# Seams of a two-layer transformer kernel cut by token tile, with the next stage's first two weight units multiplied in column halves

## What is computed

```python
for l in range(DEPTH):                       # DEPTH = 2
    # six modulation vectors per layer from silu(c) @ w_mod[l], for latents and for context
    h = rms_norm(x, g_pre_mix[l]) * (1 + sc1) + sh1
    y_lat, y_ctx = token_mixer(h, h_ctx, ...) # w_in, differential attention, gated linear attention, w_out
    x = x + gt1 * rms_norm(y_lat, g_post_mix[l])
    h = rms_norm(x, g_pre_ffn[l]) * (1 + sc2) + sh2
    f = swiglu(h, ffn_w1, ffn_w3, ffn_w2) if l == 0 else moe_ffn(h, router, moe_w1, moe_w3, moe_w2)
    x = x + gt2 * rms_norm(f, g_post_ffn[l])  # the context goes the same way in layer 0
```

## Time and profile before

| | |
|---|---|
| median of 3 runs | 2034.84 us (2032.96 to 2035.08) |
| the profiled execution | 2033.05 us |
| its span, first to last instruction | 2030.9 us |
| PE busy | 1885.3 us, 93% |
| DVE busy | 1242.8 us, 61% |
| ACT busy | 1068.4 us, 53% |
| POOL busy | 43.6 us, 2% |
| mean granted PE clock | 0.944 |

### The profile page before, as it was taken

How to read it: one execution, slowest core, us unless ns; L and a number is a source line. 1 busy time by engine, 2 the same in 40 slices (tenths; PEclk the granted TensorE clock), 3 DMA queues, 4 the chain that set the end, 5 groups by cost and what they waited for, 6 DMA issues and landing times.

```text
span 2030.9 us, 25112 instructions
## 1 busy us (share of the span) xinstructions
PE 1885.3 (93%) x10056; PEld 1536.4 (76%) x10056; DVE 1242.8 (61%) x1379; ACT 1068.4 (53%) x1368; POOL 43.6 (2%) x38
## 2 busy tenths in 40 slices
PE   6999889979999997998886999999999999999995
PEld 4877567968888786876666888888888888888784
DVE  3232752453223334433645889898989898898886
ACT  4323542352222224424634777777777777676764
POOL 0000000000000000000001020000000000000000
PEclk9999875989999999999967999999999999999997
DMA  8312643212332222223712899998999998999994
GB/s 340 104 58 72 227 156 112 83 63 83 104 104 83 104 84 83 90 82 117 278 52 115 326 351 365 344 364 343 365 343 363 345 362 347 359 344 341 351 334 163
DMA packets 61528, 441.84 MB, mean 218 GB/s; under 512 B 6836, under 2 KB 6964, under 8 KB 8288
## 3 DMA queue, kind: packets, MB, share of 16 engines
q1 hardware_dynamic: 60032, 436.23, 57.3%
q10 hardware_dynamic: 1120, 3.28, 0.4%
q0 software_dynamic: 256, 0.66, 0.1%
HBM read 439.10 MB, written 1.05 MB: 217 GB/s over the span
## 4 chain that ended last, share of the span: by engine, by line
PE 83%; DVE 10%; ACT 4%; DMA 1%; issue 1%; SPq 0%; DVEq 0%; ACTq 0%
PE psum L1447 72%; PE psum L1789 2%; DMA raw<-units 1%; PE psum L1665 1%; DVE act_lo L1089 1%; PE psum L1671 1%; PE psum L1832 1%; PE psum L1464 1%; DVE row_max L1169 1%; PE psum L1805 1%; ACT probs L774 1%; PE psum L1470 1%; DVE states L1200 1%; DVE y_mix L1238 1%; DVE act_hi L1087 1%
## 5 line engine op out<-in xcount | busy, mean ns | idle before, releaser
L1332 DVE TENSOR_TENSOR w_lo<-raw,w_hi 128x2048 fp32r<-128x2048 f32 x136 | 311.0, 2290 | 50.8 <-ACT w_hi L923 50.3
L923 ACT ACTIVATE w_hi<-raw 128x2048 fp32r<-128x2048 f32 x136 | 261.0, 1920 | 107.2 <-PE psum L1447 104.6
L1025 DVE TENSOR_TENSOR w_lo<-raw,w_hi 128x1024 fp32r<-128x1024 f32 x130 | 153.4, 1221 | 233.1 <-ACT w_hi L630 233.1
L1447 PE MATMUL psum<-w_hi,xt_hi 128*128 128x512 f32 x596 | 233.6, 392 | 2.7 <-DVE xt_lo L1337 2.7
L1447 PE MATMUL psum<-w_hi,xt_lo 128*128 128x512 f32 x596 | 232.7, 390 | 0.0
L1447 PE MATMUL psum<-w_lo,xt_hi 128*128 128x512 f32 x596 | 232.6, 390 | 0.0
L1332 DVE TENSOR_TENSOR w_lo<-raw_more,w_hi 128x2048 fp32r<-128x2048 f32 x90 | 206.0, 2290 | 34.9 <-ACT w_hi L923 34.5
L630 ACT ACTIVATE w_hi<-raw 128x1024 fp32r<-128x1024 f32 x130 | 130.2, 1051 | 156.9 <-PE psum L1447 151.5
L923 ACT ACTIVATE w_hi<-raw_more 128x2048 fp32r<-128x2048 f32 x90 | 172.9, 1921 | 74.5 <-PE psum L1447 74.5
L1447 PE MATMUL psum<-act_hi,w_hi 128*128 128x512 f32 (+1 forms) x544 | 208.4, 383 | 2.1 <-DVE act_lo L1089 1.9
L1447 PE MATMUL psum<-act_lo,w_hi 128*128 128x512 f32 (+1 forms) x544 | 207.2, 381 | 0.0
(11 more groups left out here) (260 smaller groups left out, 3505.8 us busy)
## 6 DMA issues: line engine op xcount, KB each, us to landing
raw<-units SPq DMA_DIRECT2D x295, 1024.0 KB, 4.9
raw_more<-units SPq DMA_DIRECT2D x120, 1024.0 KB, 5.0
X<-ctx_in ACTq DMA_DIRECT2D x1, 1024.0 KB, 16.4
X<-x_in ACTq DMA_DIRECT2D x1, 1024.0 KB, 23.2
out<-X SPq DMA_DIRECT2D x1, 1024.0 KB, 4.1
const<-const_in ACTq DMA_DIRECT2D x1, 520.0 KB, 9.5
rope<-rope_in POOLq DMA_DIRECT2D x2, 256.0 KB, 5.5
wsm<-wsm_in ACTq DMA_DIRECT2D x1, 288.0 KB, 26.8
```

The costliest lines, as they stand in the source:

```text
L923: act.activation(w_place(m)[0], raw_place(m), ACT.Copy).then_inc(esem("w_high"), 1)
L1025: ins = dve.tensor_tensor(w_lo[:, i % RING, part], raw[:, i % RING, part], w_hi[:, i % RING, part].bitcast(F32), ALU.subtract)
L1332: dve.tensor_tensor(lo, raw_place(m), hi.bitcast(F32), ALU.subtract).then_inc(esem("w_ready"), 1)
L1447: ins = pe.matmul(dst, lhs(a), rhs(b), start=first and n == 0, stop=last and n == 2)
```

## The change

Each seam is cut by token tile:

- `out_projection` gives each token tile its own job (`("Y", l, u, t)`). The first two units are multiplied for all tiles, the last two (`LAST_UNITS`) tile by tile. In the feed-forward the last four chunks (`LATE`) are added tile by tile too; to hold them, the last two get places of their own (`ffn_place`).
- Behind each tile's keys, ACT squares the banks with an accumulator straight from PSUM (`square`), DVE multiplies by the gate from PSUM (`gated`), reduces the partial sums, and adds the tile to `X` with the reciprocal as scalar (`tile_residual`). POOL's additions at the three seams go. Then the tile is normed; one tile later PE turns it (`turn_tile`, two jobs `TT` of four blocks each, counted apart from `filled`, hence `FILL`), ACT modulates it in 128-column pieces (`tile_modulated`), DVE splits it (`tile_low`). `seam` interleaves this: products and residual of tile n, first half of tile n-1, norm of tile n, second half of tile n-1.
- The next stage's first two units are multiplied with tiles 0 and 1 (256 columns), then with tiles 2 and 3. For layer 1 the key units are put first (`row_units`, and the same order when the weights are packed).
- The second set of gates moves: in layer 0 the context's behind the first half of the first up unit and the latents' behind the first two units; in layer 1 behind the logits and `H2`. The logits come before `H2`, and DVE's `h2_lo` after the picking.

The core of the diff:

```diff
+def row_units(l):
+    units = [(2 * u, 2 * u + 1) for u in range(IN_F)]
+    return units if l == 0 else units[2:4] + units[0:2] + units[4:]
+LAST_UNITS = 2
+LATE = 2 * LAST_UNITS
...
 # psum_jobs
-        out += [("Y", l, u, g) for u in range(OUT_UNITS) for g in range(2 if l == 0 else 1)]
-        out += [("GB", l, 1, s, h) for s in sides(l) for h in range(2)]
-        out += [("T", l, "ffn", k) for k in range(KT)]
+        out += [("Y", l, u, t) for u, t in out_order(l)]
+        out += [("TT", l, "ffn", n, half) for n in range(len(token_tiles(l, "out"))) for half in range(2)]
...
+FILL = {key: n + 1 for n, key in enumerate(key for key in JOBS if key[0] != "TT")}
...
 # POOL
-                pool.wait_ge(filled, JOBS["T", 1, "mix", 0] + 1)
+                pool.wait_ge(filled, FILL["D", 0, TILES - 1, 1])
             pool.dma_start(rope[:, :, :], rope_in).then_inc(rope_loaded, 16)
             pool.dma_start(gw2[:, :], gw2_in[l]).then_inc(gw2_loaded, 16)
-            add(l, "mix", y_mix_of)
-            if l == 0:
-                add(0, "ffn", y_ffn_of)
...
 # ACT
+        def seam(l, stage, after, next_unit):
+            tiles = token_tiles(l, "out")
+            for n, t in enumerate(tiles):
+                keys, width = seam_keys(l, stage, t)
+                square((stage, l), keys[-2], len(keys) - 2, width)
+                square((stage, l), keys[-1], len(keys) - 1, width)
+                tile_std((stage, l), n, t)
+                if n:
+                    tile_modulated(*after, n - 1, tiles[n - 1], (0,))
+                norm(*after, (n,))
+                if t == TILES - 1 and next_unit is not None:
+                    split_upto(next_unit)
+                if n:
+                    tile_modulated(*after, n - 1, tiles[n - 1], (1,))
+            tile_modulated(*after, len(tiles) - 1, tiles[-1])
...
 # DVE
+        def tile_residual(name, n, t):
+            keys, _ = seam_keys(name[1], name[0], t)
+            y = y_mix if name[0] == "mix" else y_ffn
+            dve.tensor_reduce(y_ssq[:, t:t + 1], y_part[:, t, 0:len(keys)], X_AXIS, ALU.add).then_inc(
+                sem("ssq_%s%d" % name), 1)
+            for key in keys:
+                wait_copied(dve, key)
+            dve.wait_ge(sem("post_%s%d" % name), n + 1)
+            link(dve.reciprocal(y_rstd[:, t:t + 1], y_std[:, t:t + 1]))
+            dve.scalar_tensor_tensor(X[:, t, :], y[:, t, :], y_rstd[:, t:t + 1], X[:, t, :], ALU.mult, ALU.add).then_inc(
+                x_added(name[0], name[1], t), 1)
...
+        def out_projection(l):
...
+            first = OUT_UNITS - LAST_UNITS
+            for u in range(first):
+                split_upto(U["out", l] + u + 1)
+                for t in token_tiles(l, "out"):
+                    gated(("mix", l), ("Y", l, u, t), u, D_MODEL // OUT_UNITS)
+            split_upto(U["out", l] + OUT_UNITS - 1)
+            if l == 0:
+                split_upto(U["up", 0])
+            seam(l, "mix", (l, "ffn"), U["up", 0] + 1 if l == 0 else None)
...
 # PE
+            for u in range(OUT_UNITS - LAST_UNITS):
+                for t in tiles:
+                    columns(u, t)
+            for n, t in enumerate(tiles):
+                columns(OUT_UNITS - 2, t)
+                columns(OUT_UNITS - 1, t)
+                if n:
+                    turn_tile(l, "ffn", n - 1, tiles[n - 1])
...
+            gate_up(0, 0, CTX)
+            turn_tile(0, "ffn", TILES - 1, TILES - 1)
+            gates_on_all(0, 1, (0,))
+            gate_up(1, 0, CTX)
+            gate_up(0, CTX, T)
+            gate_up(1, CTX, T)
+            gates_on_all(0, 1, (1,))
+            for j in range(2, UP_UNITS):
+                gate_up(j, 0, T)
...
+            for t in range(TILES):
+                for h in range(2):
+                    for f in range(FT - LATE, FT):
+                        if t == 0:
+                            unit(U["down", 0] + f // 2)
+                            pe.wait_ge(sem("ffn_lo"), f + 1)
+                        ins = product(f, t, h)
+                    ins.then_inc(filled, 1)
+                if t:
+                    turn_tile(1, "mix", t - 1, t - 1)
...
+            if l == 1:
+                rows(0, 0, CTX, tiles_ready(CTX // P))
+                turn_tile(1, "mix", TILES - 1, TILES - 1)
+                rows(1, 0, CTX, tiles_ready(CTX // P))
+                rows(0, CTX, T, tiles_ready(TILES))
+                rows(1, CTX, T, tiles_ready(TILES))
```

More of the change, by code:

```diff
@@ new lines, in _, with seam @@
+        products = {}
+        def seam(l, stage, after, next_unit):
+            tiles = token_tiles(l, "out")
+            for n, t in enumerate(tiles):
+                keys, width = seam_keys(l, stage, t)
+                gated((stage, l), keys[-2], len(keys) - 2, width)
+                gated((stage, l), keys[-1], len(keys) - 1, width)
+                tile_residual((stage, l), n, t)
+                if n:
+                    tile_low(*after, n - 1, tiles[n - 1], (0,))
+                norm(*after, (n,))
+                if t == TILES - 1 and next_unit is not None:
+                    split_upto(next_unit)
+                if n:
+                    tile_low(*after, n - 1, tiles[n - 1], (1,))
+            tile_low(*after, len(tiles) - 1, tiles[-1])
@@ L1311, in _ @@
         dve.tensor_tensor(field(TAKEN), field(FIRST), field(SECOND), ALU.add).then_inc(sem("taken"), 1)
+        for q in range(4):
+            key = ("H2", q)
+            part = slice((q % 2) * 512, (q % 2 + 1) * 512)
+            dve.wait_ge(sem("h2_hi"), q + 1)
+            empties(dve.tensor_tensor(h2_lo[:, q // 2, part], bank(key), h2_hi[:, q // 2, part].bitcast(F32),
+                                      ALU.subtract), key)
         dve.wait_ge(sem("top_exp"), 1)
@@ L1499, in turn, with turn_tile @@
                 ins.then_inc(filled, 1)
+        def turn_tile(l, stage, n, t):
+            pe.wait_ge(sem(f"xn_{stage}{l}"), n + 1)
+            for half in range(2):
+                key = ("TT", l, stage, n, half)
+                wait_emptied(pe, key)
+                for k in range(4 * half, 4 * half + 4):
+                    ins = pe.transpose(bank(key)[:, (k % 4) * P:(k % 4 + 1) * P], xn[:, t, k * P:(k + 1) * P], ident)
+                ins.then_inc(sem(f"turned_{stage}{l}"), 1)
         def gate_logits(l):
@@ L1713, in dense_ffn, with product @@
                     wait_emptied(pe, ("D", 0, t, h))
-            for f in range(FT):
-                s = unit(U["down", 0] + f // 2)
+            def product(f, t, h):
+                s, c0 = (U["down", 0] + f // 2) % RING, (f % 2) * D_MODEL + h * 512
+                return three(bank(("D", 0, t, h)), lambda a: ffn_place(a, f)[:, t * P:(t + 1) * P],
+                             lambda b: weights[b][:, s, c0:c0 + 512], f == 0, f == FT - 1)
+            for f in range(FT - LATE):
+                unit(U["down", 0] + f // 2)
                 pe.wait_ge(sem("ffn_lo"), f + 1)
```

292 lines of the change are left out of this document (179 added, 113 removed).

## The result

The changed kernel takes **2004.3 us** (median of four runs, 2003.8 to 2007.7) against 2035.0 for the kernel before, measured beside it: ratio 0.985, 95% interval 0.984 to 0.987, 27 to 33 us faster. The forecast was 1998, with a range of 1991 to 2007. The sign and the range held. Executions of one kernel differ by 3 to 8 us.

The account below looks back on a forecast made before the run. PE is busy 93% of the span, so time can only come from seams where it waits on serial ACT-DVE chains. Gains 14.8 + 14.4 + 7.6 = 36.8 from 2033.05 give 1996.3; plus 1.8 for the median, 1998 us, range 1991 to 2007.

Parts of the forecast that it names:

- A: Seam from layer 0's attention output to feed-forward, with a PE hole of 24.6 us: cutting by tile gains 14.8 us.
- the stall: In the output projection, PE waits 0.7 us for DVE's late split of the fourth output unit.
- B: Seam from layer 0's feed-forward to layer 1, with a PE hole of 24.1 us: cutting by tile gains 14.4 us.
- its waits: PE's stalls at B, on chunk 19, tile 0's xn, the loop and the second unit's split: 4.2 us together.
- the handover loop: ACT and DVE's chain per tile at B: 7.5 us against PE's 6.5 us of work.
- the first rival: At all three seams the ACT-DVE handover becomes the bound: gain 25 to 29 us, 2006 to 2010 us; chance 0.17.
- C: Seam from layer 1 to the experts: routing ready 18.4 us after the last key against 26.7, gaining 7.6 us.
- All hides: Rival at the three seams: only order-fixed stalls remain, narrow Identities take 0.28; gain 43.6 us, 1991 us; chance 0.06.
- Waits only move: Rival: banks or ring places held by the other column half keep A's and B's holes; 2026 to 2034 us; chance 0.03.
- The clock in the tile phases: Rival: brief waits halve PE's clock across 90.8 us of tails and half keys at A and B; 2089 us; chance 0.04.
- The row at 679.95: Profile row of a 2.3 us PE wait followed at once by 0.23 us products, cited against the clock falling.
- The rule that I quoted: Brief idles between matmul groups can make PE's clock swing between its levels; by it the clock rival would hold.

Follow-up runs that it names:

- Experiment 6: Changed kernel with only the last two chunks of the down products added tile by tile instead of four: 2009.5 us.
- Experiment 1: Changed kernel with PE multiplying 36 blocks that nobody reads while it waits for the last tile's xn at C: 2001.2 us.
- experiment 3: Changed kernel with layer 1's second gates, then 20 blocks that nobody reads, put ahead of the last tile's transposes at C: 2001.1 us.
- experiment 2: Changed kernel with layer 1's second gates (PE's broadcast and ACT's two copies) moved ahead of the last tile's transposes at C: 2001.2 us.
- 8: Changed kernel with the edits of experiment 3 and experiment 7 (40 blocks in layer 1), an earlier fourth-output-unit split, and unread blocks before four modulation steps: 1969.8 us.
- 9: The kernel of 8 without the two fillings beside attention (44 and 42 blocks): 1968.0 us, 0.968 of the kernel before.
- 10: Changed kernel without column halves and with layer 1's input projection in the old order, query units first: 2023.1 us.
- experiment 7: Changed kernel with unread blocks (20 in layer 0, 56 in layer 1) in PE's wait for gated linear attention's first masked block: 1985.9 us.

## Why the prediction was right, and where it was short

- **A** held: 15.4 against 14.8. The rates (2.88 a key, 0.37 the narrow Identity, no wait but one) are in the trace; the stall was 0.4 and a tile's transposes 0.80 on PE's path in place of 1.04.
- **B** held: 13.9 against 14.4, with its waits where they were listed. In part the nearness is luck: the seam brought 15.6, of which about 1 comes from before's low clock behind its hole, and a drop of the clock that I had not counted took 1.6 back. Experiment 6 shows that the handover loop (7.29 us, forecast 7.5) is the bound here, the first rival's mechanism at the forecast's price.
- **C** is the step that failed. I wrote of the transposes "I take 0.13 where PE comes from work", knew the wait of 4.7 us and the low clock behind seam C, and kept the clock out of C's sum: the transposes, the logits, the turn-back and the gates stood at full pace. (Only the positions stood at 2.3, before's row at the low clock; they took 1.18.) Logits ended 14.3 us behind the last key and not 10.8; the later gate copies held ACT's exponential back to 21.8 in place of 16.9; routed came at 23.3 in place of 18.4. Experiment 1 takes 4.0 of these 4.9 back by the clock alone, experiment 3 all of them.
- **Outside the seams** I had no loss. 1.6 us went at the gate logits, 1.2 with the execution, 0.4 at the fourth output unit, 0.9 in the experts' stage. That stage has waits of 2.73 us at its first product, of 2.12 near 782 us and of 2.12 some 101 us later. Of the 0.9, 1.3 come behind the last of them: PE ends its products at the same distance, but DVE starts its last low part (`ey_lo`) over 1 us later, for a reason that I did not find; 0.3 are won at the start. Experiments 1 and 2 (900.8 and 900.6) don't show the loss, since in their traces the clock does not fall behind the last wait of 2.12, as it does in before and after. In 3, 8, 9 and 10, which take 3 to 4 us more than before, it falls behind the first wait of 2.12 too (0.50 from 1865.4 to 1868.4 in experiment 3), which costs 1.6 us, and it stays low longer at the start, which costs about 1. Why it falls in one trace and not in another is open.
- **The rivals.** All hides: no, B's loop doesn't. Waits only move: no. The clock in the tile phases: no; waits of up to 1.3 us left it at 1.00 at A and B. Its mechanism was right at C, to which I had given no rival. The row at 679.95, my evidence against it, did not carry that far: behind the same wait the changed kernel's clock did fall, for some 3.4 us. The rule that I quoted from the Trainium skill, "TensorE: Matmul & The Clock Gate", section "A second HAM failure mode: psum-queue depth-cycling", is not borne out by the tile phases of A and B; the drops behind the waits of 2.33 and 2.12 us agree with it.

## What to carry to other kernels

When a serial handover between stages is cut by tile, price the last tile by itself: where no other work covers it, as at C, PE's clock fell behind the wait, so the small products there cost up to twice as much, on the path that sets the end. A wait on PE in front of many small products is worth an experiment that fills it with products that nobody reads, cut to the wait's length. Here it paid for waits of 1.95 to 7.78 us where PE set the pace, and brought nothing that shows beside attention (5.48 and 5.29 us); with two reorderings it was worth 36 us, more than the change itself. Keep copies that nobody is waiting for out of the way of a table load and its function (1.7 us, experiment 3 against 1). Read effects of a few us from the stage between two events, not from the total, and look at the clock behind every wait of that stage before you give the effect to the edit.

## What was not expected of the hardware

- The clock stays low long after the wait: some 20 us in layer 1's gated linear attention (0.50 from 999.3 to 1018.8 us, PE busy throughout) and 60 us in layer 0's (292 to 352, PE busy in 57.1 of them with small products; its two waits are 0.52 us at 323 and 2.38 us at 329). With the wait filled the same products run at 1.00 and in layer 1 need 1.41 in place of 2.54 us a step.
- The clock can drop for 3.4 us in a stretch where PE has no gap at all, in every trace with the change and in neither of before. The Trainium skill's page "TensorE: Matmul & The Clock Gate", section "What's actually happening", says that the moment of the switch varies from run to run of one kernel; the 1.2 us between after's two traces agree with that, while the drop itself came in each of them.
- Waits of up to 1.3 us between long runs of keys left the clock at 1.00 (A and B). Behind one of 2.86 us (experiment 2) and two of 1.95 and 2.57 us between small products (layer 0's linear attention, experiment 7) it fell.
- The same wait between the same 512-column products can do either. Behind 2.33 us ahead of the first down product the clock stayed at 1.00 in both traces of before and three with the change, and fell to 0.50 for some 3.4 us, which cost 1.6, in the nine others.
